# Pieces 0 to 3 of x loaded through ScalarE's DMA queue in a one-core decoder layer

## The chip, the cores and the metric

The kernel runs on 1 core of a Trainium2 chip. A core has a matrix engine (TensorE, PE in the profile), VectorE (DVE), ScalarE (ACT), GpSimd (POOL) and SyncE (SP), and DMA engines that all of them share. Each engine runs its own list of instructions in order, and the lists meet only through semaphores. A load is an instruction in the list of the engine that issues it; it finishes later, by itself, and raises a semaphore. The metric is the device time of one execution in microseconds, as the median of several runs.

## What is computed

One decoder layer over 256 tokens of width 2048, in float32. The start of it matters here: all of x is multiplied by the input weights, head by head.

```python
proj = jnp.einsum('bsd,dc->bsc', x, w_in[l]).astype(f32)       # x: (1, 256, 2048)
q_a, k_a, v_a, q_b, k_b, v_b = jnp.split(proj, splits, axis=-1)
q_a = apply_rope(q_a...); k_a = apply_rope(k_a...)
o_a = diff_attention(q_a, k_a, v_a, lam, subln_g[l], lambda_init)
...
o_b = dilated_attention(q_b, k_b, v_b)
attn_out = jnp.einsum('bsc,cd->bsd', mix, w_out[l])
x = layer_norm(DEEPNORM_ALPHA * x + attn_out, ln1_g[l], ln1_b[l])
hdn = jnp.square(jax.nn.relu(jnp.einsum('bsd,df->bsf', x, w_ff1[l])))
ff_out = jnp.einsum('bsf,fd->bsd', hdn, w_ff2[l])
x = layer_norm(DEEPNORM_ALPHA * x + ff_out, ln2_g[l], ln2_b[l])
```

## The kernel before

**Units.** The 2048 rows of a weight matrix are taken in 8 units of 256 rows (`KU` = 2 blocks of 128). For one head a unit is 256 x 384 numbers (q, k and v of the head), 384 KB, loaded by two instructions of 192 KB (L263). Units go round four buffers, `SLOTS` = 4, of `w_raw`. Unit k of head 0 is called unit k below; units 8 and up are the next head's.

**Three products for one.** To keep float32 precision each operand is split in a rounded part and a rest. ScalarE rounds `w_raw` to `w_hi` (L646), VectorE subtracts to get `w_lo` (L893), and TensorE adds three products, hi x hi, hi x lo, lo x hi (L366, L368, L370). A unit of a head takes 12 of them, for 2 blocks of rows and 2 tiles of tokens.

**x.** x comes in 8 pieces of 256 columns, 256 KB each (L277), into `y1`, which the profile calls `y`. TensorE transposes a piece by four instructions (`transpose_x`, L341) against the identity, itself a load of 64 KB at the very start (L1332). ScalarE rounds the transposed piece to `xT_hi` (L667) and VectorE makes `xT_lo` (L911). Unit k needs piece k.

**What sets the order.** The order is written out by hand. TensorE, in `head_slot`, first does 6 warm-up products on zeros (`WARM_UP`, L331), transposes piece 0, 2 warm-ups, piece 1, 2 warm-ups, then unit 0; then pieces 2 and 3, then unit 1; then one piece ahead of each of the next four units. ScalarE and VectorE take, in turn, piece k and unit k for the first four. A piece's bank of PSUM is used again four pieces later.

**SyncE's queue.** SP issues in turn: piece 0, unit 0, piece 1, unit 1 and so on to piece 7, unit 7. Units 0 to 3 wait for nothing. From unit 4 on, a unit's load waits for the semaphore `w_split`, raised when the unit four before it has been split (`load_head_unit`, L259). Whatever is behind it on SP waits too.

**GpSimd** starts its loads (`lam_in`, then `tables`, which the rope of L933 to L940 needs) once TensorE has finished unit 1. The first rope, its sum `qk` (L940) and the transposes of it on TensorE (L409) come in the second head's turn, after its unit 1.

**ScalarE's queue** issues no load at all in this version. Its first instruction loads the table of activation functions.

Of the kernel before, what the change touches and what calls it, by code (L numbers as in the profile page):

```python
# [20 lines left out]
P = 128  # L21
# [16 lines left out]
KU = 2  # L38
SLOTS = 4
# [65 lines left out]
def hybrid_layer(nc, x, w_in, lq1, lk1, lq2, lk2, subln_g, w_out, ln1_g, ln1_b, w_ff1, w_ff2,  # L105
# [5 lines left out]
    def at(name, shape, dtype, offset):  # L111
        return nc.alloc_sbuf_tensor_at(name, shape, dtype, offset=base + offset)
# [43 lines left out]
    y1 = at("y1", [P, TT, D_MODEL], F32, A0 + 24 * KB)  # L156
# [44 lines left out]
    def sem(name):  # L201
        sems[name] = nc.alloc_semaphore(name)
        return sems[name]
# [6 lines left out]
    x_loaded = [sem(f"x_loaded{k}") for k in range(UPH)]  # L210
# [27 lines left out]
    x_d = x.rearrange("b (t p) d -> p (b t) d", p=P)  # L238
# [16 lines left out]
    def load_head_unit(sp, kind, h, head, k, first_lap=False):  # L255

        slot = k % SLOTS
        if not first_lap:
            sp.wait_ge(w_split, UPH * h + k - (SLOTS - 1))  # L259
        dst = w_raw[:, slot, 0:KU * HC].rearrange("p (k s d) -> p k s d", k=KU, s=3)  # L260
        for kk in range(KU):
            src = w_in_d[:, k, kk, kind, :, one(head), :].rearrange("p s h d -> p s (h d)")
            sp.dma_start(dst[:, kk], src).then_inc(w_loaded[slot], 16)  # L263

    def load_chunk_unit(sp, w, u, row, chunk, slot, back=SLOTS):

        sp.wait_ge(w_split, u - (back - 1))
        dst = w_raw[:, slot, :].rearrange("p (k n) -> p k n", k=KU)
        src = w[:, row, :, chunk, :] if isinstance(chunk, int) else (
            w[:, row, :, one(chunk), :].rearrange("p k c n -> p k (c n)"))  # L270
        sp.dma_start(dst, src).then_inc(w_loaded[slot], 16)

    def sync_program(sp):

        for k in range(UPH):
            cols = slice(k * KU * P, (k + 1) * KU * P)
            sp.dma_start(y1[:, :, cols], x_d[:, :, cols]).then_inc(x_loaded[k], 16)  # L277
            load_head_unit(sp, 0, 0, 0, k, first_lap=k < SLOTS)
        for kind in range(2):
            first = 1 if kind == 0 else 0  # L280
            with sp.Fori(first, N_DIFF) as j:
                for k in range(UPH):
                    load_head_unit(sp, kind, j + N_DIFF * kind, j, k)
        with sp.Fori(0, CHUNKS - 1) as n:
            for k in range(UPH):
                load_chunk_unit(sp, w_out_d, UPH * n + (U_OUT + k), k, n, k % SLOTS)

        sp.wait_ge(w_used, U_OUT + UPH)
        for k in range(SLOTS):
            sp.dma_start(side_raw[:, k, :].rearrange("p (k n) -> p k n", k=KU),  # L290
                         w_ff1_d[:, k, :, 0, :]).then_inc(side_loaded[k], 16)
        for k in range(UPH):
            load_chunk_unit(sp, w_out_d, U_OUT + UPH * (CHUNKS - 1) + k, k, CHUNKS - 1, k % SLOTS)
        for k in range(SLOTS, UPH):
            load_chunk_unit(sp, w_ff1_d, U_FF1 + k, k, 0, k % SLOTS, back=2 * SLOTS)
        with sp.Fori(1, CHUNKS_FF) as n:
            for k in range(UPH):
                load_chunk_unit(sp, w_ff1_d, UPH * n + (U_FF1 + k), k, n, k % SLOTS)
        with sp.Fori(0, CHUNKS - 1) as n:
            with sp.Fori(0, UPF // SLOTS) as lap:  # L300
                for k in range(SLOTS):
                    load_ff2_unit(sp, UPF * n + SLOTS * lap + (U_FF2 + k), SLOTS * lap + k, n, k)
        for k in range(UPF):
            load_ff2_unit(sp, U_FF2 + UPF * (CHUNKS - 1) + k, k, CHUNKS - 1, k % SLOTS)
            if k == UPF * 3 // 4:

                sp.wait_ge(w_used, U_FF2 + UPF * (CHUNKS - 1) + UPF // 2)
                for n, v in enumerate((ln2_g, ln2_b)):
                    sp.dma_start(ln2_gb[:, n, :], v.partition_broadcast(P).rearrange(
                        "p l d -> p (l d)")).then_inc(gb2_loaded, 16)  # L310
        for i, (tt, cols) in enumerate(LAST_PIECES):
            sp.wait_ge(y2_ready, i + 1)
            sp.dma_start(out_d[:, tt, cols], y2[:, tt, cols]).then_inc(stored, 16)
        sp.wait_ge(stored, 16 * len(LAST_PIECES))

    def load_ff2_unit(sp, u, row, chunk, slot):
        sp.wait_ge(w_split, u - (SLOTS - 1))
        dst = w_raw[:, slot, :].rearrange("p (k n) -> p k n", k=KU)
        if isinstance(row, int):
            src = w_ff2_d[:, row, :, chunk, :]  # L320
        else:
            src = w_ff2_d[:, one(row), :, one(chunk), :].rearrange("p u k c n -> p (u k) (c n)")
        sp.dma_start(dst, src).then_inc(w_loaded[slot], 16)
# [310 lines left out]
    def scalar_program(act):  # L634
        def round_unit(u, slot, lap, cols, fresh=False, back=SLOTS, units=1):

            if cols == KU * HC:
                loads = KU * lap  # L640
            else:
                loads = lap + (KU - 1) * (U_OUT // SLOTS)
            act.wait_ge(w_loaded[slot], 16 * loads)
            if not fresh:
                act.wait_ge(w_used, u - (back - 1))
            act.activation(w_hi[:, slot, 0:cols], w_raw[:, slot, 0:cols], ACT.Copy).then_inc(  # L646
                w_rounded, units)
# [16 lines left out]
        def round_x(i):  # L664

            act.wait_ge(turned, i + 1)
            act.activation(xT_hi[:, i * KU:(i + 1) * KU, :].rearrange("p k t -> p (k t)"),  # L667
                           piece_ps[i % 4], ACT.Copy).then_inc(turn_rounded, 1)
# [34 lines left out]
        def scale_output(h):  # L703
            act.wait_ge(scale_ready, h + 1)
            for tt in range(TT):
                ins = act.activation(o_sb[:, tt, :], out_ps[:, 0, tt * P:(tt + 1) * P], ACT.Copy,
                                     scale=o_scale[:, tt:tt + 1])
            ins.then_inc(o_ready, 1)
# [12 lines left out]
        def slot(h, parity, att_maps, out_maps):  # L721
# [23 lines left out]
            if att_maps == 2:  # L745
                scale_output(h - 1)

        for k in range(SLOTS):
            round_x(k)
            round_unit(k, k, 1, KU * HC, fresh=True)  # L750
# [578 lines left out]
    with nc.Block() as block:  # L1329
        @block.sync  # L1330
        def _(sp):
            sp.dma_start(ident_t[:, :], table[:, 0:P]).then_inc(ident_loaded, 16)  # L1332
            sync_program(sp)

        @block.tensor
        def _(pe):
            tensor_program(pe)

        @block.scalar
        def _(act):  # L1340
            scalar_program(act)

        @block.vector
        def _(dve):
            vector_program(dve)

        @block.gpsimd
        def _(pool):
            gpsimd_program(pool)
# [19 lines left out]
```

## Time and profile before

| | us |
|---|---|
| median of 3 runs | 1130.5 |
| lowest and highest | 1129.39, 1130.81 |
| the profiled execution | 1129.92 |
| its span, first to last instruction | 1128.1 |
| TensorE busy with products | 1112.4 |
| VectorE busy | 654.3 |
| ScalarE busy | 506.2 |

Times in the profile count from the start of the span. A row of the view in order of time gives the start, the length, the engine, the line, what is written and read, and in brackets how long the engine had been idle and what ended it. `PEld` is TensorE's loading of the stationary operand, `SPq` SyncE issuing a load; the length of such a row is the issuing, not the transfer. Rows with x4 or x12 are merged from as many instructions. Matmuls are pipelined, so one row's length is more than its distance to the next.

### The profile page before, as it was taken

How to read it: one execution, taken by the hardware profiler on the slowest of the kernel's cores; microseconds unless marked ns; L12 is line 12 of the kernel's file. 1: busy time of each engine (PE TensorE's matmuls, PEld its weight loads, DVE VectorE, ACT ScalarE, POOL GpSimd, SP SyncE). 2: the span in 40 equal slices, each digit the busy share in tenths (PEclk: the TensorE clock that was granted, in tenths of full speed). 3: DMA queues.
4: the chain of work that ended last, by engine and by line, in shares of the span. 5: the costliest groups of instructions: out<-in, count | busy, mean ns of one | idle time of the engine just before them, and what ended most of it. 6: DMA issues, size and time to landing. Idle time of an engine off the chain costs nothing.

```text
span 1128.1 us, 16832 instructions
## 1 busy us (share of the span) xinstructions
PE 1112.4 (99%) x5884; PEld 981.6 (87%) x5884; DVE 654.3 (58%) x737; ACT 506.2 (45%) x676; POOL 25.6 (2%) x53
## 2 busy tenths in 40 slices
PE   9999999999999999999999999999999999999996
PEld 8999999999988878888888888888888888888885
DVE  5666666665655685566556555655445445445446
ACT  4555555444543434444445444444333343343341
POOL 1000000000000010000000000000000000000001
PEclk9999999999999999999999999999999999999998
DMA  9655557655565855666666666667666666656672
GB/s 264 187 154 165 166 167 229 180 162 175 164 201 170 282 173 163 188 188 187 199 187 186 187 190 191 182 195 263 198 194 191 197 190 193 197 190 194 193 264 93
DMA packets 185764, 215.42 MB, mean 191 GB/s; under 512 B 9281, under 2 KB 110017, under 8 KB 185089
## 3 DMA queue, kind: packets, MB, share of 16 engines
q1 hardware_dynamic: 184352, 207.72, 60.5%
q0 software_dynamic: 1376, 7.21, 1.9%
q8 instruction: 25, 0.41, 0.1%
q14 instruction: 11, 0.08, 0.0%
HBM read 210.70 MB, written 4.19 MB: 190 GB/s over the span
## 4 chain that ended last, share of the span: by engine, by line
PE 95%; DVE 2%; DMA 2%; issue 1%; SPq 0%; ACT 0%; POOL 0%; POOLq 0%; DVEq 0%
PE low_ps L574 11%; PE high_ps L370 10%; PE high_ps L368 10%; PE high_ps L366 10%; PE low_ps L366 10%; PE low_ps L370 10%; PE low_ps L368 10%; PE high_ps L574 9%; PE low_ps L579 5%; PE high_ps L579 5%; PE high_ps L419 1%; PE high_ps L442 1%; PE high_ps L409 1%; DMA w_raw<-in_w_in 1%; DMA y<-in_x 1%
## 5 line engine op out<-in xcount | busy, mean ns | idle before, releaser
L893 DVE TENSOR_TENSOR w_lo<-w_raw,w_hi 128x1024 fp32r<-128x1024 f32 (+1 forms) x408 | 462.5, 1140 | 373.0 <-ACT w_hi L646 372.5
L646 ACT ACTIVATE w_hi<-w_raw 128x1024 fp32r<-128x1024 f32 (+1 forms) x408 | 403.9, 992 | 495.9 <-PE high_ps L370 191.9
L366 PE MATMUL high_ps<-w_hi,hidT_hi 128*128 128x512 f32 x480 | 186.8, 389 | 0.0
L370 PE MATMUL high_ps<-w_hi,hidT_lo 128*128 128x512 f32 x480 | 186.8, 389 | 0.0
L368 PE MATMUL high_ps<-w_lo,hidT_hi 128*128 128x512 f32 x480 | 186.8, 389 | 0.0
L366 PE MATMUL low_ps<-w_hi,xT_hi 128*128 128x384 f32 x512 | 179.0, 350 | 0.0
L574 PE MATMUL low_ps<-x1T,w_hi 128*128 128x512 f32 x512 | 176.8, 394 | 0.7 <-ACT relu L830 0.7
L370 PE MATMUL low_ps<-w_hi,xT_lo 128*128 128x384 f32 x512 | 171.8, 336 | 0.0
L368 PE MATMUL low_ps<-w_lo,xT_hi 128*128 128x384 f32 x512 | 171.7, 335 | 0.0
L574 PE MATMUL high_ps<-x1T,w_hi 128*128 128x512 f32 x448 | 155.0, 394 | 0.0
L579 PE MATMUL low_ps<-x1T,w_lo 128*128 128x256 f32 x512 | 137.0, 278 | 0.0
L579 PE MATMUL high_ps<-x1T,w_lo 128*128 128x256 f32 x448 | 119.9, 278 | 0.0
L574 PEld LDWEIGHTS low_ps<-x1T,w_hi 128*128 128x128 f32 x512 | 94.4, 188 | 20.4 <-ACT relu L830 1.1
L368 PEld LDWEIGHTS high_ps<-w_lo,hidT_hi 128*128 128x128 f32 x480 | 90.1, 188 | 18.8
L366 PEld LDWEIGHTS high_ps<-w_hi,hidT_hi 128*128 128x128 f32 x480 | 90.1, 188 | 18.7
L370 PEld LDWEIGHTS high_ps<-w_hi,hidT_lo 128*128 128x128 f32 x480 | 90.1, 188 | 18.6
L366 PEld LDWEIGHTS low_ps<-w_hi,xT_hi 128*128 128x128 f32 x512 | 96.4, 188 | 3.1 <-issue 2.7
L579 PEld LDWEIGHTS low_ps<-x1T,w_lo 128*128 128x128 f32 x512 | 96.2, 188 | 2.8
L574 PEld LDWEIGHTS high_ps<-x1T,w_hi 128*128 128x128 f32 x448 | 82.6, 188 | 17.2
L368 PEld LDWEIGHTS low_ps<-w_lo,xT_hi 128*128 128x128 f32 x512 | 96.5, 188 | 0.2
L370 PEld LDWEIGHTS low_ps<-w_hi,xT_lo 128*128 128x128 f32 x512 | 96.1, 188 | 0.0
L579 PEld LDWEIGHTS high_ps<-x1T,w_lo 128*128 128x128 f32 x448 | 84.2, 188 | 2.5
(134 smaller groups left out, 810.0 us busy)
## 6 DMA issues: line engine op xcount, KB each, us to landing
w_raw<-in_w_ff SPq DMA_DIRECT2D x252, 512.0 KB, 3.7
w_raw<-in_w_in SPq DMA_DIRECT2D x256, 192.0 KB, 2.7
w_raw<-in_w_out SPq DMA_DIRECT2D x32, 512.0 KB, 4.8
y<-in_x SPq DMA_DIRECT2D x8, 256.0 KB, 5.5
side_raw<-in_w_ff SPq DMA_DIRECT2D x4, 512.0 KB, 6.9
ln_spill<-y POOLq DMA_DIRECT2D x8, 256.0 KB, 3.4
y<-ln_spill POOLq DMA_DIRECT2D x1, 2048.0 KB, 10.3
ln_gb<-in_ln_g POOLq DMA_DIRECT2D x1, 1024.0 KB, 6.1
```

The lines of the kernel that those rows point to most:

```text
L366: pe.matmul(acc[:, tt, 0:cols], hi[:, toks], right_hi[:, slot, w], start=(t == 0), stop=False)
L368: pe.matmul(acc[:, tt, 0:cols], hi[:, toks], right_lo[:, slot, w], start=False, stop=False)
L370: ins = pe.matmul(acc[:, tt, 0:cols], lo[:, toks], right_hi[:, slot, w], start=False, stop=(t == kts - 1))
L409: ins = pe.transpose(turn_ps[:, 0, s * SEQ + tt * P:s * SEQ + (tt + 1) * P], qk[:, tt, s * P:(s + 1) * P], ident_t[:, :])
L419: ins = pe.matmul(scores_ps[:, m, keys_of(tt)], qkT[rows, 0, tt * P:(tt + 1) * P], qkT[rows, 1, 0:(tt + 1) * P], start=True, stop=True)
L442: ins = pe.matmul(out_ps[:, 0, first:first + P], left, right, start=(key_tile == 0), stop=(key_tile == tt))
L574: return pe.matmul(banks[:, b, :], w_hi[:, slot, cols], x1T[:, t, :, :].rearrange("p h t -> p (h t)"), start=(t == 0), stop=(t == KT - 1))
L579: return pe.matmul(banks[:, b, 0:SEQ], w_lo[:, slot, cols], x1T[:, t, 0, :], start=False, stop=False)
L646: act.activation(w_hi[:, slot, 0:cols], w_raw[:, slot, 0:cols], ACT.Copy).then_inc(w_rounded, units)
L893: dve.tensor_tensor(w_lo[:, slot, 0:cols], w_raw[:, slot, 0:cols], w_hi[:, slot, 0:cols].bitcast(F32), ALU.subtract).then_inc(w_split, units)
```

## The change

The four loads of pieces 0 to 3 move from SyncE's list to the head of ScalarE's. SyncE issues units 0 to 3 one after the other and goes on with piece 4. All other instructions, waits and buffers stay; each piece still raises its own semaphore.

```diff
+    def load_x(queue, k):
+
+        cols = slice(k * KU * P, (k + 1) * KU * P)
+        queue.dma_start(y1[:, :, cols], x_d[:, :, cols]).then_inc(x_loaded[k], 16)
+
     def sync_program(sp):
 
         for k in range(UPH):
-            cols = slice(k * KU * P, (k + 1) * KU * P)
-            sp.dma_start(y1[:, :, cols], x_d[:, :, cols]).then_inc(x_loaded[k], 16)
+            if k >= SLOTS:
+                load_x(sp, k)
             load_head_unit(sp, 0, 0, 0, k, first_lap=k < SLOTS)
...
+        for k in range(SLOTS):
+            load_x(act, k)
         for k in range(SLOTS):
             round_x(k)
             round_unit(k, k, 1, KU * HC, fresh=True)
```

The start of SyncE's list, as a difference (- before, + after; `y_80` is the buffer of x, `x8` means eight such rows in a row; the lines of the changed kernel lie a few higher):

```order
-L1332 DMA ident_t<-in_table 128x128
-L277 DMA y_80<-in_x 128x2x256
+L1339 DMA ident_t<-in_table 128x128
+L263 DMA w_raw<-in_w_in 128x3x128 x8
+L276 DMA y_80<-in_x 128x2x256
 L263 DMA w_raw<-in_w_in 128x3x128 x2
-L277 DMA y_80<-in_x 128x2x256
+L276 DMA y_80<-in_x 128x2x256
```

The eight loads of units 0 to 3 now stand in one block behind the identity, and the first x on this list is piece 4.

The start of ScalarE's list before:

```order
L1339 UNCONDITIONAL_BRANCH
L667 ACT_TABLE_LOAD
L667 ACTIVATE xT_hi<-high_ps 128x512
L646 ACTIVATE w_hi<-w_raw 128x768
```

And after:

```order
L1346 UNCONDITIONAL_BRANCH
L276 DMA y_80<-in_x 128x2x256 x4
L672 ACT_TABLE_LOAD
L672 ACTIVATE xT_hi<-high_ps 128x512
L651 ACTIVATE w_hi<-w_raw 128x768
```

Four loads of x stand ahead of the table load; the rounding work behind it keeps its order. TensorE's, VectorE's and GpSimd's lists are the same.

## Rows read from the trace of the kernel before

**Rows 1.** The page: busy time of TensorE; shares of the last chain; the loads of x

```profile
PE 1112.4 (99%) x5884; PEld 981.6 (87%) x5884; DVE 654.3 (58%) x737; ACT 506.2 (45%) x676; POOL 25.6 (2%) x53
...
PE 95%; DVE 2%; DMA 2%; issue 1%; SPq 0%; ACT 0%; POOL 0%; POOLq 0%; DVEq 0%
...
y<-in_x SPq DMA_DIRECT2D x8, 256.0 KB, 5.5
```

**Rows 2.** The granted clock of the core over the whole span

```profile
core 0: 1128.1 us, clock 0.997
```

**Rows 3.** Waits of TensorE, whole program: us in total, times, longest

```profile
PE high_ps L341 <- DMA y<-in_x: 1.4, 2, 0.8
...
PE high_ps L409 <- DVE qk L940: 0.9, 1, 0.9
```

**Rows 4.** In order of time, 0 to 20 us: TensorE, ScalarE, VectorE

```profile
1.06 2.93 PE L331 MATMUL low_ps<-zeros 128*128 128x128 f32 x12 [1.06 <-DVE zeros L1019]
...
4.82 1.09 PE L341 MATMUL high_ps<-ident_t,y 128*128 128x128 f32 x4 [0.83 <-DMA y<-in_x]
...
6.43 0.83 ACT L646 ACTIVATE w_hi<-w_raw 128x768 fp32r<-128x768 f32 x1
...
6.86 1.12 PE L341 MATMUL high_ps<-ident_t,y 128*128 128x128 f32 x4
7.30 0.96 DVE L893 TENSOR_TENSOR w_lo<-w_raw,w_hi 128x768 fp32r<-128x768 f32 x1
...
8.48 0.55 PE L366 MATMUL low_ps<-w_hi,xT_hi 128*128 128x384 f32 x1
...
9.02 0.85 ACT L646 ACTIVATE w_hi<-w_raw 128x768 fp32r<-128x768 f32 x1 [0.41 <-DMA w_raw<-in_w_in]
...
10.78 0.60 PE L341 MATMUL high_ps<-ident_t,y 128*128 128x128 f32 x4
...
11.90 0.66 PE L341 MATMUL high_ps<-ident_t,y 128*128 128x128 f32 x4 [0.53 <-DMA y<-in_x]
...
12.32 0.42 PE L366 MATMUL low_ps<-w_hi,xT_hi 128*128 128x384 f32 x1
...
19.54 0.60 PE L341 MATMUL high_ps<-ident_t,y 128*128 128x128 f32 x4
```

**Rows 5.** In order of time: ScalarE's first instruction and SyncE's issues

```profile
0.74 1.28 ACT L667 ACT_TABLE_LOAD   x1 [0.74 <-PEq L1360]
...
1.18 0.42 SPq L277 DMA_DIRECT2D y<-in_x  x1
1.65 0.99 SPq L263 DMA_DIRECT2D w_raw<-in_w_in  x2
...
12.54 0.90 SPq L277 DMA_DIRECT2D y<-in_x  x1
```

**Rows 6.** The last chain, 0 to 45 us: start, length, what

```profile
5.84 6.02 DMA y<-in_x
...
20.67 0.84 ACT w_hi L646
...
23.22 7.09 DMA w_raw<-in_w_in
...
34.22 0.66 PE high_ps L409 x4
```

**Rows 7.** Piece 0 alone (issued 1.18): time from issue to landing

```profile
DMA to landing us min/median/max: 3.5/3.5/3.5
```

**Rows 8.** Unit 0's two loads (issued 1.65 and 2.16): the second landed last

```profile
DMA to landing us min/median/max: 3.2/3.4/3.6
```

**Rows 9.** Unit 1's second load alone, issued 3.73

```profile
DMA to landing us min/median/max: 5.3/5.3/5.3
```

**Rows 10.** Queues, 22.5 to 25.5 us: packets, MB, share; q0 is GpSimd's, q1 SyncE's

```profile
q0 software_dynamic: 157, 0.66, 57.5%
q1 hardware_dynamic: 760, 0.37, 43.0%
```

## The prediction

> **What bounds the kernel now.** I read the page first: TensorE has work in 99% of the span and makes 95% of the chain that ended last, while transfers make 2% [rows 1]. A change to loads can therefore only act where TensorE waits for one. The waits of TensorE come next: for pieces of x there are two in the whole program, 1.4 us together, the longer one 0.8; later there is one of 0.9 us for `qk`, the result of the first rope [rows 3]. Then the start in order of time [rows 4], where the reader should see two meeting paths. One is x: its piece 0 is transposed at 4.82, piece 1 at 6.86, then warm-up products, and the first product of unit 0 comes at 8.48. The other is the weights: unit 0 is rounded by ScalarE at 6.43 and split by VectorE from 7.30 to 8.26. They arrive within 0.2 us of each other, so either one alone can delay unit 0. Unit 0 then runs until 10.78. Piece 2 is transposed at once, piece 3 only at 11.90, since it landed at 11.86 [rows 6], and unit 1 starts at 12.32. From there each unit follows the last without a wait (such transposes come at 19.54, for piece 6). So what can be won before unit 1 is the wait for piece 3; the earlier wait, 0.8 us before 4.82, lies ahead of a path that has to be kept short on both sides.
>
> **The clock at the start.** The granted clock reads 0.997 over the span [rows 2]. The lengths are plainer: four transposes take 1.09 and 1.12 us at 4.82 and 6.86, and 0.60 at 10.78 [rows 4]. TensorE is at the lower of its two levels (1.2 GHz) until about 8.4 and at 2.4 GHz after it, having been busy most of the time since 1.06.
>
> **What the change takes away.** SP no longer issues pieces 0 to 3, four instructions of 0.42 us (piece 0's) to 0.5 (half of the 0.99 for two weight loads), 1.7 to 2.0 us in all [rows 5]. Nothing computes on SP, and its issuing runs ahead of the landing: piece 3 is issued at 5.84 and lands 6.02 us later [rows 6], piece 0 lands 3.5 us after its issue [rows 7]. The saved issue time is thus worth only the start. Unit 0's two loads, issued from 1.65, can start at about 1.2; piece 0, issued at 1.18, can start at 0.74, where ScalarE's first instruction stands [rows 5]. That is a lead of 0.44 us.
>
> **What it adds.** ScalarE issues four loads ahead of its table load. At SP's own 0.5 us each that is 2.0 us; the table load of 1.28 us then ends at 4.0 instead of 2.0 [rows 5]. ScalarE's first work, rounding piece 0, comes after the transposes, about 5.9, so 1.9 us of cover remain. It is gone if one issue takes over 0.98 us. A gain is excluded, since no later work starts sooner by it. I count 0.
>
> **What it moves: whose bytes come first.** The same bytes are loaded. Units carry 384 KB, pieces of x 256 KB, the identity 64. From the landings before: 704 KB (identity, piece 0, unit 0) at 2.16 + 3.6 = 5.8 [rows 8]; 1344 KB (with piece 1 and unit 1) at 3.73 + 5.3 = 9.0 [rows 9]; 2240 KB (with piece 2, unit 2, piece 3) at 11.86. Between these I interpolate, 196 and 317 KB per us. Now two queues are full at once and share the DMA engines. How they share is not in the start of this trace. The nearest rows are those where GpSimd's queue and SP's are both full, 22.5 to 25.5: 157 packets with 0.66 MB against 760 packets with 0.37 MB, 57.5% against 43.0% of the engines' time [rows 10]. The number of packets is far from equal, the time is nearly so. I take equal bytes for x (packets of 1 KB) and weights (512 B), with the 0.44 us of lead:
> - Unit 0 ends its queue's first 448 KB, so 896 KB in all: 6.74 - 0.44 = 6.3. ScalarE rounds it at 6.43 as before: no delay.
> - Piece 1 ends 512 KB of x, 1024 KB in all: 7.4 - 0.44 = 7.0 against 6.86. Unit 0's first product moves by 0.1 to 8.6, its end to 10.9.
> - Piece 3 ends x, by then 832 to 1024 KB of weights may be in too: at most 1856 to 2048 KB, 10.2 to 10.8 instead of 11.86. It no longer makes TensorE wait. The two sets of transposes, 0.35 and 0.42 us (10.78 and 11.90 show such sets; 11.90 to 12.32 is one), follow unit 0: unit 1 can start at 11.7.
> - Unit 1 is through with 1664 to 1856 KB: 9.6 to 10.2 against 9.0, later. Rounding 0.85 and splitting 0.96 [rows 4] with 0.1 between put its split at 11.5 to 12.1. This is what is late next, in place of piece 3.
> So unit 1 starts at 11.7 to 12.1 instead of 12.32: **0.2 to 0.6 us earlier; I take 0.5**, near the equal shares.
>
> **The queue behind the waits.** Pieces 4 to 7 stay on SP, each in front of a unit that waits for an earlier split. Unit 5 waits for unit 1's split, which moves from 10.9 to about 11.5 or 12, and piece 6 is queued behind it. Piece 6 was issued at 12.54 [rows 5], pieces take a median 5.5 us to land [rows 1], and its transposes came at 19.54 [rows 4]: 1.5 us of slack, of which the later issue takes 0.6 to 1.2 and the earlier TensorE 0.5. I count 0, up to +0.3. Piece 4 is issued earlier than before, behind the same bytes: 0.
>
> **What becomes of it.** The next stretch in which TensorE waits is at 34.22, 0.9 us for the rope [rows 3], whose chain runs through a weight load of 7.09 us [rows 6]. If that chain doesn't come forward, TensorE waits longer there and the gain is gone: between 0 and -0.5. The chain begins with the rounding at 20.67 [rows 6], which follows the transposes of a piece of x, and GpSimd's loads start at the end of unit 1, so both move with TensorE; I keep -0.5. Of a delay the same wait could swallow up to 0.9. After that no load is waited for by TensorE [rows 3], so the shift goes to the end.
>
> **Sum.** The profiled execution took 1129.92 us (span 1128.1). 1129.92 - 0.5 = 1129.4. That execution lies 0.6 below the median of the three runs, so the median should be 1130.0.
>
> The Trainium skill speaks against the change: DMA: Bandwidth & Descriptors, section Rules for kernel authors, says that spreading loads over the issuing engines doesn't raise bandwidth and saves issue time alone. Where issue time isn't waited for, that gives no change, 1130.5; the trace agrees that it isn't waited for, but the order of the bytes is another matter, and on that my half microsecond rests.
>
> **Rivals.**
> *A, the loads still come in order of issue.* Then the change hardly does what it says: unit 0's second load stands behind two or three pieces, 960 to 1216 KB, 6.6 to 7.9. From rounding to first product it took 8.48 - 6.43 = 2.05, so unit 0 starts at 8.7 to 9.9, ends 2.3 later, and after 0.8 of transposes unit 1 starts at 11.8 to 13.0; with unit 1 landed at 10.2 not before 12.1. That is -0.2 to +0.7: 1130.3 to 1131.2. For it: every row of the start shows that order on one queue. Against it: rows 10.
> *B, slower: x crowds out unit 0.* If the queues take turns by packets of equal number, x gets two bytes for each byte of weights. Unit 0 lands behind 448 KB and 896 KB of x: 9.0 - 0.44 = 8.6. It starts at 10.65 (+2.2), unit 1 at 13.8 (+1.5). From about 8.4 to 10.65 TensorE then has nothing to do, directly at the point where its clock rises. With the clock up this is +0.6 (0.9 swallowed) to +1.5: 1131.1 to 1132.0. If it is down for unit 0, the twelve products that take 2.3 us (8.48 to 10.78) take twice that, +2.3: +2.9 to +3.8, or 1133.4 to 1134.3. The mechanism begins once unit 0 lands after 6.4, and costs over 0.2% when it also takes the clock. For it: the wait for both paths leaves no slack. Against it: the counts of rows 10, one to five.
> The skill's same page, section Queues, rings and completion order, has each DMA engine take turns between queues packet by packet; read as equal counts of descriptors that is B's time, while rows 10 show the counts unequal.
> *C, faster:* two queues fill the engines sooner. Without the waits of 0.8 and 0.5 us, and with the lead, at best -1.3: 1129.2. No step here reaches -2.3.
>
> **How the numbers follow.** This kernel can be told from no change at about 0.2%, 2.3 us. Chances: forecast 0.45; A 0.25; B with the clock up 0.13; B with it down 0.12; C 0.02, and 0.03 for something in the start that I don't see. Same takes the forecast, A, C and B with the clock up, 0.85, less 0.03 for a larger gain than I see: 0.82. Slower is B with the clock down and two thirds of the unseen, 0.14. Faster is that 0.03 and the last third, 0.04. The likeliest gives 1130.0, its own bounds (0 to -0.6, medians of three runs differing by some 0.7) 1129.2 to 1131.2. The range leaves out the lower clock: 1128.8 to 1132.4.
>
> **What would show it.** Right: pieces 0 to 3 on ScalarE from 0.74; no wait for x before the transposes of piece 3; unit 0's first product at 8.4 to 8.7; unit 1's at 11.7 to 12.1, held by VectorE's split; the wait for the rope still 0.8 to 1.0. Wrong: ScalarE rounding unit 0 after 7 us because of a transfer (A or B), first products of 0.35 us spacing instead of 0.17 (the clock), or the rope's wait taking up the shift.

## The result

| | before | changed |
|---|---|---|
| median of 15 runs each, us | 1130.5 | 1132.11 |
| lowest and highest | 1129.1, 1131.65 | 1130.87, 1134.44 |
| ratio, 95% interval | | 1.0019 (1.0012 to 1.0026) |
| profiled execution, its span | 1129.92, 1128.1 | 1133.35, 1131.6 |

The changed kernel is 1.6 us slower; a gain of 0.5 was predicted. It was measured twice more, later: 1.0003 (0.9993 to 1.0012, which holds no change) and 1.0015 (1.0005 to 1.0024). So the loss lies between 0.6 and 1.6 us by the medians and between 0.3 and 2.1 by the ratios, and a difference that small needs many runs. In two of the three measurements its executions also spread more than those of before.

The start of the changed kernel in order of time, to be laid beside [rows 4] and [rows 5] (start, length, engine, line, operation, what ended the idle time; `ACTq` is ScalarE issuing):

```profile
0.73 2.04 ACTq L276 DMA_DIRECT2D y<-in_x  x4
...
1.18 6.80 SPq L263 DMA_DIRECT2D w_raw<-in_w_in  x8
2.81 1.28 ACT L672 ACT_TABLE_LOAD   x1 [2.81 <-issue]
...
4.39 1.09 PE L346 MATMUL high_ps<-ident_t,y 128*128 128x128 f32 x4 [0.41 <-DMA y<-in_x]
...
6.63 0.66 PE L346 MATMUL high_ps<-ident_t,y 128*128 128x128 f32 x4 [0.42 <-DMA y<-in_x]
...
7.12 0.61 PE L336 MATMUL low_ps<-zeros 128*128 128x128 f32 x4
...
8.50 0.84 ACT L651 ACTIVATE w_hi<-w_raw 128x768 fp32r<-128x768 f32 x1 [2.38 <-DMA w_raw<-in_w_in]
...
9.38 0.96 DVE L900 TENSOR_TENSOR w_lo<-w_raw,w_hi 128x768 fp32r<-128x768 f32 x1 [2.54 <-ACT w_hi L651]
...
10.48 0.66 PE L371 MATMUL low_ps<-w_hi,xT_hi 128*128 128x384 f32 x1 [2.75 <-DVE w_lo L900]
...
11.26 0.52 PE L375 MATMUL low_ps<-w_hi,xT_lo 128*128 128x384 f32 x1
...
11.58 0.52 PE L371 MATMUL low_ps<-w_hi,xT_hi 128*128 128x384 f32 x1
...
14.46 1.89 PE L346 MATMUL high_ps<-ident_t,y 128*128 128x128 f32 x8
...
16.02 0.50 PE L371 MATMUL low_ps<-w_hi,xT_hi 128*128 128x384 f32 x1
```

Three things differ from [rows 4]. First, ScalarE waits 2.38 us for unit 0 and rounds it at 8.50 instead of 6.43. Second, TensorE therefore stands idle for 2.75 us until 10.48 (before: 8.48, no wait). Third, the products of unit 0 come 0.32 us apart (11.26 to 11.58), not 0.17, so the unit takes until 14.46: 4.0 us instead of 2.3. The two sets of transposes behind it wait for nothing, as intended, but at the slow rate they take 1.56 us. Unit 1 begins at 16.02 instead of 12.32, **3.7 us later**.

TensorE's clock by stretch (the column after the five engines is the granted clock, 1.00 being 2.4 GHz; then the share of the DMA engines and GB/s):

```profile
5.00:10.00 5.00, 2.32 (x15) 1.94 (x13) 1.31 (x2) 1.93 (x3) 0.00 (x0) 0.94 1.07 307
10.00:15.00 5.00, 4.52 (x15) 4.45 (x16) 1.89 (x3) 0.84 (x1) 0.00 (x0) 0.50 1.10 302
15.00:20.00 5.00, 5.00 (x31) 4.97 (x30) 3.59 (x5) 3.65 (x6) 0.93 (x2) 0.88 0.46 137
```

Here the column shows it: 0.50, the lower level, from 10 to 15 us. The transposes of piece 1 at 6.63 took 0.66 us, so the clock had already been up, and it fell while TensorE was idle: 0.94 over 5 to 10 us is 0.6 us at the lower level, which puts the fall near 9.4, some 1.7 us after the last product on zeros. The column must be read with care. It reads 1.00 from 0 to 5 us too, where four transposes took 1.09 us, and in e9 from 10 to 15 us, where products are 0.32 us apart: the trace has no record of the clock before its first change, which in e9 is the rise at 13.6 us. The spacing of the products is the surer sign.

The waits of TensorE, against [rows 3]: us in total, times, longest.

```profile
PE low_ps L371 <- DVE w_lo L900: 3.1, 2, 2.7
...
PE high_ps L346 <- DMA y<-in_x: 0.8, 2, 0.4
...
PE high_ps L414 <- DVE qk L947: 0.3, 1, 0.3
```

The wait for x shrank from 1.4 to 0.8, the new wait for unit 0's split is 2.7, and the rope's wait gave back 0.6 (0.9 to 0.3), half of which a new 0.3 us wait for a split shortly before it (at 33.09) took again. The profiled execution grew by 3.4 us. So nearly the whole shift of unit 1 reached the end.

### The profile page after: what moved, and what is told of

Same layout as the page of the kernel before. It is cut to its first block, busy times and chain, and to the rows that moved or that the text cites. A ratio compares the mean times of both kernels' runs of the same rounds, so it can differ in the third digit from the quotient of the medians.

```text
span 1131.6 us, 16832 instructions
## 1 busy us (share of the span) xinstructions
PE 1114.2 (98%) x5884; PEld 983.3 (87%) x5884; DVE 654.1 (58%) x737; ACT 506.4 (45%) x676; POOL 25.6 (2%) x53
## 4 chain that ended last, share of the span: by engine, by line
PE 95%; DVE 2%; DMA 2%; issue 1%; ACT 0%; POOL 0%; SPq 0%; POOLq 0%; DVEq 0%
PE low_ps L579 10%; PE low_ps L371 10%; PE high_ps L373 10%; PE high_ps L371 10%; PE high_ps L375 10%; PE low_ps L375 10%; PE low_ps L373 10%; PE high_ps L579 9%; PE low_ps L584 5%; PE high_ps L584 5%; DMA w_raw<-in_w_in 1%; PE high_ps L424 1%; PE high_ps L447 1%; PE high_ps L414 1%; DMA w_raw<-in_w_out 0%
```

## The experiments

All kernels ran beside the kernel before on the same chip. In the table, "rounded" is when ScalarE starts on unit 0, "first" TensorE's first product of unit 0, "spacing" the distance of its products, "unit 1" the first product of unit 1, all from the profile of one execution; the ratio is of many runs (7 to 15 of each version).

| kernel | rounded | first | spacing | unit 1 | span | ratio (95%) |
|---|---|---|---|---|---|---|
| before | 6.43 | 8.48 | 0.17 | 12.32 | 1128.1 | 1 |
| changed | 8.50 | 10.48 | 0.32 | 16.02 | 1131.6 | 1.0019 (1.0012, 1.0026) |
| changed again, e9 | 8.65 | 10.64 | 0.32, late 0.17 | 14.95 | 1131.4 | 1.0003 (0.9993, 1.0012) |
| changed, e12 | 8.09 | 10.07 | 0.32, late 0.17 | 14.56 | 1129.7 | 1.0015 (1.0005, 1.0024) |
| x first, one queue, e1 | 9.82 | 11.80 | 0.32 | 16.32 | 1131.6 | 1.0032 (1.0020, 1.0043) |
| changed, more warm-up, e2 | 7.66 | 9.64 | 0.18 | 12.62 | 1128.3 | 0.9999 (0.9990, 1.0009) |
| the same, e13 | 7.72 | 9.70 | 0.17 | 12.65 | 1128.2 | 0.9997 (0.9988, 1.0006) |
| changed, no warm-up, e14 | 7.25 | 9.23 | 0.32 | 14.12 | 1128.8 | 1.0021 (1.0011, 1.0031) |
| x in 512 B rows, e3 | 7.29 | 9.38 | 0.32 | 14.26 | 1132.3 | 1.0018 (1.0009, 1.0028) |
| x in 8 loads, 1 KB rows, e4 | 7.39 | 9.37 | 0.18 | 13.31 | 1129.1 | 1.0001 (0.9991, 1.0010) |
| weights on ScalarE, e6 | 8.89 | 10.87 | 0.32 | 16.41 | 1132.5 | 1.0023 (1.0013, 1.0032) |
| x3 before unit 2, e7 | 5.92 | 7.89 | 0.17 | 11.46 | 1127.4 | 0.9999 (0.9990, 1.0009) |
| before, no warm-up, e8 | 5.74 | 8.68 | 0.32 | 13.58 | 1129.4 | 0.9997 (0.9988, 1.0007) |
| two pieces, e5 | 6.79 | 8.77 | 0.18 | 11.74 | 1127.2 | 0.9993 (0.9984, 1.0003) |
| two pieces again, e10 | 6.75 | 8.73 | 0.17 | 11.70 | 1127.7 | 1.0000 (0.9991, 1.0009) |
| two pieces, 4 warm-ups, e11 | 6.83 | 8.81 | 0.17 | 11.76 | 1126.4 | 0.9994 (0.9985, 1.0003) |
| the same, e15 | 6.98 | 8.97 | 0.17 | 11.92 | 1128.1 | 0.9991 (0.9982, 1.0000) |

### The changed kernel once more

> The changed kernel once more, on the same chip and in the same rounds as the two below. Theory (late unit 0 plus, in part of the executions, the lower clock): unit 0 lands at 7.6 to 8.6, behind three pieces of x; median 1131.5 to 1132.5, spread over 3 us, as before. Rival (the first measurement was a matter of the chip): median within 0.5 us of the kernel before.

Unit 0 landed at 8.63, at the edge of what was expected, but the median of 11 runs, 1131.1, was only 0.6 above the kernel before in those rounds, and the interval holds no change. Both the theory's range and the rival's were missed by a little. The executions lay from 1129.8 to 1133.2, those of before from 1128.9 to 1132.4, so no single profile stands for the median.

### Order or queue: x first on one queue

```diff
+        for k in range(SLOTS):
+            load_x(k)
         for k in range(UPH):
-            cols = slice(k * KU * P, (k + 1) * KU * P)
-            sp.dma_start(y1[:, :, cols], x_d[:, :, cols]).then_inc(x_loaded[k], 16)
+            if k >= SLOTS:
+                load_x(k)
             load_head_unit(sp, 0, 0, 0, k, first_lap=k < SLOTS)
```

> The kernel before, still with SyncE's queue alone, but with pieces 0 to 3 of x issued ahead of units 0 to 3. It puts the order of the bytes apart from the second queue. Theory (unit 0 is late because bytes of x come ahead of it): unit 0 stands behind 64 + 1024 KB, 1472 KB with itself, lands near 9.4 us, and its first product comes near 11.5; TensorE is idle for over 3 us before it, its clock is at the lower level for unit 0, and the time is 1133 to 1135. Rival (it is the second queue that costs, by contention or by ScalarE's issuing): unit 0 lands by 7 us or the time stays within 0.5 us of 1130.5.

The theory held. Without any second queue, unit 0 landed at 9.80 and the time was 0.32% above the kernel before, the worst of all.

```profile
9.82 0.84 ACT L652 ACTIVATE w_hi<-w_raw 128x768 fp32r<-128x768 f32 x1 [4.09 <-DMA w_raw<-in_w_in]
...
11.80 0.66 PE L372 MATMUL low_ps<-w_hi,xT_hi 128*128 128x384 f32 x1 [4.75 <-DVE w_lo L899]
```

It is thus enough that bytes of x come ahead of unit 0.

### How the two queues share: size of packets or size of loads

```diff
+        if k < SLOTS:
+            for c in range(KU):
+                half = slice((k * KU + c) * P, (k * KU + c + 1) * P)
+                queue.dma_start(y1[:, :, half], x_d[:, :, half]).then_inc(x_loaded[k], 16)
```

(the wait becomes 32 for these pieces; the control splits by `tt` instead: `y1[:, tt, cols]`, rows of 1 KB)

> The changed kernel, with each of pieces 0 to 3 loaded by two instructions of 128 columns, so that x comes in packets of 512 B as the weights do. Theory (the two queues take turns by something close to packets, and x wins by its larger ones): x and weights get equal bytes while both queues are full, unit 0 lands near 6.5 to 7.2 instead of 8.5, time 1130.0 to 1131. Rival (turns by instruction or by bytes): packet size changes nothing, unit 0 lands near 8.5 as in the changed kernel. The table load on ScalarE ends near 6.1 instead of 4.1, which may hold the rounding of piece 0 by 0.6 us.

> Control of the run with 512 B packets: each of pieces 0 to 3 is loaded by two instructions as well, one for each tile of tokens, with packets of 1 KB as in the changed kernel. Theory (packets): x gets more bytes than the weights, unit 0 lands at 8.0 to 8.6 and the time is as the changed kernel's, near 1132. Rival (the number of instructions or ScalarE's slower issue decides): unit 0 lands as early as in the run with 512 B packets.

The theory of packets fell. Queue lines for 3 to 6 us (packets, MB, share of the DMA engines; q10 is ScalarE's queue with x, q1 SyncE's with the weights), first of the changed kernel:

```profile
q10 hardware_dynamic: 533, 0.52, 53.9%
q1 hardware_dynamic: 747, 0.37, 45.3%
```

With x in loads of 128 KB and packets of 512 B:

```profile
q1 hardware_dynamic: 908, 0.45, 52.2%
q10 hardware_dynamic: 619, 0.30, 37.6%
```

With x in loads of 128 KB and packets of 1 KB:

```profile
q1 hardware_dynamic: 1017, 0.50, 57.8%
q10 hardware_dynamic: 405, 0.37, 39.6%
```

The bytes of x to those of the weights are 1.4, 0.67 and 0.74 to 1. The sizes of one load of each are 256 to 192 (1.33), 128 to 192 (0.67) and 128 to 192. The size of a packet, doubled between the last two, moved little. The shares follow the size of a load, as if the queues took turns load by load. With the queues exchanged (e6, below) they still do over the same 3 us: x, now on q1, has loads of 256 KB and 1.6 times the bytes.

```profile
q1 hardware_dynamic: 521, 0.50, 56.9%
q10 hardware_dynamic: 646, 0.32, 36.3%
```

Both engines issue a load in 0.49 us, one after the other, so turns by load can't be told here from plain order of issue.

Shares alone don't give the landing. A load raises its semaphore sixteen times, and the trace holds the time of each. Of the 32 signals of unit 0's two loads, the 24th came at 5.16 us in the kernel before and at 6.2 to 6.4 in the six profiles with the changed kernel's loads. The last one, which is the landing, came at 5.80 before and at 7.2 to 8.6 in those six. In the changed kernel's own profile 31 of the 32 had come by 6.79 and the last at 8.48, after piece 2 (7.68). With two pieces on ScalarE's queue (e5) the 24th came at 5.95 and the last at 6.76. So about 1.1 us of the late landing is in the bulk of the bytes, and the rest, 0.2 to 1.7 us, differs from execution to execution and lies in the last few signals. What delays those is not shown.

Both expectations missed in part. With 512 B rows unit 0 landed at 7.19, as its theory said, but the median was 1132.87 instead of 1130 to 1131. In the control it landed at 6.42 instead of 8.0 to 8.6, so its rival held; ScalarE rounded it only at 7.39, since it had issued eight loads and its table load ended at 6.9.

The medians are a different matter: with 512 B rows the time was no better than the changed kernel's, although unit 0 was rounded at 7.29. Piece 1 landed at 7.7 there and was transposed at 7.75, the table load ended late (6.8), and unit 0 ran at the lower clock. A version can cure one delay and meet another.

### The queues exchanged

```diff
+        for k in range(SLOTS):
+            load_head_unit(act, 0, 0, 0, k, first_lap=True)
         for k in range(SLOTS):
             round_x(k)
```

> The queues exchanged: units 0 to 3 (8 loads of 192 KB) on ScalarE's queue, all pieces of x on SyncE's. Theory (turns by whole load, whichever engine issues): order of landing as in the changed kernel, unit 0 near 7.7 to 8.5. ScalarE now issues 8 loads, over 4 us, so its table load ends after 6 us and the rounding of piece 0 begins near 6.5: time 1131 to 1134. Rival (SyncE's queue is served last, ScalarE's first): unit 0 lands by 6 us.

Right in the time, wrong in the landing. Unit 0's halves were now the first and third load to be issued and landed by 6.4; no engine's queue is served last. What held unit 0 in this profile was ScalarE itself, which issued for 6.34 us before it could load its table:

```profile
0.73 6.34 ACTq L263 DMA_DIRECT2D w_raw<-in_w_in  x8
7.11 1.28 ACT L668 ACT_TABLE_LOAD   x1 [7.11 <-issue]
8.40 0.60 ACT L668 ACTIVATE xT_hi<-high_ps 128x512 fp32r<-128x512 f32 x1
8.89 0.84 ACT L647 ACTIVATE w_hi<-w_raw 128x768 fp32r<-128x768 f32 x1
```

The last three of these loads took 0.8 to 1.6 us to issue instead of 0.5: the cover that the prediction counted for ScalarE's issues does run out, with eight loads.

### The clock: work for TensorE in the wait

```diff
-WARM_UP = (6, 2, 2)
+WARM_UP = (6, 2, 9)
```

> The changed kernel with 9 warm-up products on zeros ahead of unit 0 instead of 2, so that TensorE has work until about 9.5 us. Theory (part of the loss is TensorE's clock, which falls during the wait for unit 0): unit 0's products stand 0.17 us apart instead of 0.32, its first product stays near 10.5, and the median is 1131.0 to 1131.5, with no run over 1133. Rival (the loss is the late landing alone, the clock only goes with it): spacing or median unchanged within 0.3 us of 1132.1, or worse by the products added.

> The changed kernel, beside the next two. Theory (landing alone costs 0.3 to 0.8 us at the end, the clock up to 2 more in part of the executions): median 0.5 to 1.6 us above the kernel before. Rival (landing alone): all executions 0.3 to 0.8 us above it.

> The changed kernel with 9 instead of 2 warm-up products ahead of unit 0. Theory (clock): median at least 0.5 us below the changed kernel's in the same rounds, and the slowest executions, over 1132.5, gone. Rival (no clock): as the changed kernel, or slower.

> The changed kernel with no warm-up products at all, so that TensorE does nothing but two sets of transposes until unit 0 at about 10.5 us. Theory (clock): all of unit 0 and often part of unit 1 at the lower level in every execution, median 1132.5 to 1134, 1 us or more above the changed kernel. Rival: no different from the changed kernel, as the kernel before showed no difference without its warm-up.

The first run showed the loss gone, but in another session than the changed kernel's. e12, e13 and e14 ran side by side. Medians: 1131.51, 1129.95 and 1132.31, beside 1130.2 for the kernel before. The slowest executions were 1135.8, 1130.6 and 1134.5. Seven useless products more make the changed kernel 1.6 us faster. Without any, e14 was only 0.8 us above e12, less than the 1 us and more that was expected. With the seven, of e13:

```profile
6.11 0.66 PE L346 MATMUL high_ps<-ident_t,y 128*128 128x128 f32 x4 [0.25 <-DMA y<-in_x]
...
6.60 2.17 PE L336 MATMUL low_ps<-zeros 128*128 128x128 f32 x18
...
7.72 0.84 ACT L651 ACTIVATE w_hi<-w_raw 128x768 fp32r<-128x768 f32 x1 [1.67 <-DMA w_raw<-in_w_in]
...
9.70 0.41 PE L371 MATMUL low_ps<-w_hi,xT_hi 128*128 128x384 f32 x1 [0.93 <-DVE w_lo L900]
10.12 0.34 PE L375 MATMUL low_ps<-w_hi,xT_lo 128*128 128x384 f32 x1
10.30 0.33 PE L371 MATMUL low_ps<-w_hi,xT_hi 128*128 128x384 f32 x1
...
12.65 0.42 PE L371 MATMUL low_ps<-w_hi,xT_hi 128*128 128x384 f32 x1
```

Unit 0 is still 1.2 us late (9.70), its products are 0.17 us apart, and unit 1 is only 0.3 late, since it no longer waits for piece 3. That is the price of the order of bytes alone, and by the ratio of 0.9997 it can't be told from nothing. The rest of the loss goes with the clock, whether it falls in the wait or hasn't risen by then: in e9 and e12 the transposes of piece 1, at 6.7 and 6.8, still took 1.12 us. e12, the same loads without the added products, has unit 1 at 14.56, 1.9 later:

```profile
6.79 1.12 PE L346 MATMUL high_ps<-ident_t,y 128*128 128x128 f32 x4 [0.63 <-DMA y<-in_x]
```

But the two profiles differ before the added products begin. The kernels are the same up to there, and yet in e13 (and e2) the clock was already up at 6.11, in e12 not at 6.79. So the pair shows what the two states of the clock are worth, 1.9 us at unit 1. That the products keep it up is shown by the medians and the slowest executions, and once more by e10 and e11 below (two and four products, medians 1130.1 and 1129.4), not by these profiles. The profiled execution of e14 was its fastest run (1130.54), which is why its span looks better than its ratio.

The Trainium skill (TensorE: Matmul & The Clock Gate, section What's actually happening) has the array throttled by default, at half its clock, until activity releases it. The trace agrees in the two levels: spacings of 0.32 and 0.17 us.

> The kernel before, all loads as they were, without any of the warm-up products on zeros. It puts the price of TensorE's clock apart from the landings. Theory (of the changed kernel's loss some 2 us are the clock): unit 0 lands as before, its products stand 0.32 us apart, unit 0 takes 4.0 us instead of 2.3 and perhaps part of unit 1 too, time 1131.5 to 1133. Rival (the clock costs little, since the wait for piece 3 and the rope's wait take it up): within 0.5 us of 1130.0.

The kernel before without its warm-up products (`WARM_UP = (0, 0, 0)`): in the profile unit 0 ran at the lower clock and unit 1 began 1.3 us late, the wait for piece 3 having swallowed the rest. The profiled execution took 1131.27, but the median was that of the kernel before (1130.3 to 1130.2): the rival held, not the theory of 1131.5 to 1133.

```profile
7.92 1.12 PE L341 MATMUL high_ps<-ident_t,y 128*128 128x128 f32 x4 [2.70 <-DMA y<-in_x]
8.68 0.67 PE L366 MATMUL low_ps<-w_hi,xT_hi 128*128 128x384 f32 x1
...
13.58 0.42 PE L366 MATMUL low_ps<-w_hi,xT_hi 128*128 128x384 f32 x1
```

Why the median doesn't show the 1.3 us stays open: one profile doesn't say how often the clock is down, in either kernel. It is the one run that speaks against a price of the clock.

### Is the gain to be had without the loss?

> The kernel before with SyncE's queue alone and one exchange: piece 3 of x is issued ahead of unit 2 instead of behind it. It asks whether the gain that the change was predicted to make (no wait for piece 3 after unit 0) is to be had without touching unit 0. Theory (landing in order of issue): unit 0 as before, first product near 8.5; piece 3 lands behind 1856 KB, near 10.7, so its transposes follow piece 2's at once and unit 1 starts near 11.7 instead of 12.32, time 0.3 to 0.6 us below the kernel before. Rival: unit 2, now later, or the rope's wait at 34 us takes it up and the time is unchanged.

On one queue, with piece 3 issued ahead of unit 2:

```profile
11.46 0.42 PE L372 MATMUL low_ps<-w_hi,xT_hi 128*128 128x384 f32 x1
...
14.45 0.66 PE L347 MATMUL high_ps<-ident_t,y 128*128 128x128 f32 x4 [0.66 <-DMA y<-in_x]
14.86 0.42 PE L372 MATMUL low_ps<-w_hi,xT_hi 128*128 128x384 f32 x1
```

Unit 1 began at 11.46, 0.9 earlier. Of this 0.6 is not the exchange: unit 0 had begun at 7.89 instead of 8.48, with the clock already up for piece 0 (its transposes took 0.63 us). Then TensorE waited for piece 4, and unit 2 began at 14.86 (kernel before: 14.84). The gain was turned into the next wait, and the median didn't move. The rival was right.

> The changed kernel with only pieces 0 and 1 on ScalarE's queue; pieces 2 and 3 go back to SyncE, ahead of units 2 and 3. The runs so far show landings in turns of whole loads, one from each queue: piece 0, first half of unit 0, piece 1, (piece 2,) second half of unit 0. Theory (turns by whole load): with no piece 2 on that queue, unit 0 is whole behind 64 + 512 + 384 = 960 KB and lands near 6.6 to 7.1 instead of 7.7 to 8.5; first product near 9.0, clock up in most executions, median 1129.8 to 1130.8. Rival (any second queue delays unit 0 as much): landing near 8, median near 1132.

> Pieces 0 and 1 on ScalarE's queue, 2 and 3 on SyncE's, for an interval that can tell 0.8 us. Theory: unit 1 begins at 11.7 instead of 12.3 and the shift goes to the end, 0.5 to 0.9 us below the kernel before. Rival: the first 0.8 us was noise or is taken up by the rope's wait, and the difference is under 0.3 us.

> The same with 4 instead of 2 warm-up products before unit 0, in the 1.1 us in which TensorE waits for unit 0's split. Theory (the clock still falls there in some executions): fewer slow executions, median 0.2 to 0.5 us lower than with two. Rival: with landing near 6.8 the clock holds anyway, and four products at the lower clock take 2.1 us and delay unit 0 by 0.3 us: same or up to 0.3 us more.

> Pieces 0 and 1 on ScalarE, 4 warm-up products ahead of unit 0, once more. Theory: 0.5 to 1.0 us below the kernel before. Rival: within 0.3 us of it.

```diff
-            if k >= SLOTS:
+            if k >= 2:
                 load_x(sp, k)
...
-        for k in range(SLOTS):
+        for k in range(2):
             load_x(act, k)
```

With pieces 0 and 1 alone on ScalarE's queue (e5):

```profile
6.79 0.84 ACT L651 ACTIVATE w_hi<-w_raw 128x768 fp32r<-128x768 f32 x1 [0.48 <-DMA w_raw<-in_w_in]
...
8.77 0.41 PE L371 MATMUL low_ps<-w_hi,xT_hi 128*128 128x384 f32 x1 [1.15 <-DVE w_lo L900]
...
11.74 0.42 PE L371 MATMUL low_ps<-w_hi,xT_hi 128*128 128x384 f32 x1
...
14.29 0.42 PE L371 MATMUL low_ps<-w_hi,xT_hi 128*128 128x384 f32 x1
```

This is the timing that the prediction gave the full change: unit 1 at 11.7, and unit 2 at 14.3, 0.55 ahead of the kernel before, so in this profile the gain outlasts the next unit. In the time it isn't shown: two measurements gave 0.9993 and 1.0000, both intervals hold no change, and the second is what its rival said. With two more warm-up products (e11, e15) it was 0.9994 and 0.9991 (0.9982 to 1.0000). By the ratios that last version is 0.7 to 1.0 us faster than the kernel before (medians 1129.4 and 1129.2 against 1130.5 and 1130.2), at the edge of what can be told.

## Why the prediction was right or wrong

1130.0 was predicted and 1132.11 measured: inside the range of 1128.8 to 1132.4, but in the other direction. That it lies inside is owed to the rivals that the range took in, since the forecast's own mechanism allowed no loss, and in part to luck: the lower clock, which the profiles show, was left out of it.

- **What bounds the kernel, and where a load can act:** right. Nearly all of the difference was made before unit 1. That nothing of slack lay between unit 0's landing and its first product was right too, and proved to be the decisive row.
- **ScalarE's cover for four issues:** right. They took 2.04 us together and the table load ended at 4.1; with eight loads (e6) the cover was gone.
- **How two full queues share the DMA engines:** this is the step that failed. From [rows 10] equal bytes for both queues were taken, which gave unit 0's landing as 6.3 and no delay. It landed at 7.2 to 8.6 in six profiles with these loads. The rows don't even say so: their time is nearly equal, 57.5% to 43.0%, but their bytes are 0.66 to 0.37, 1.8 to 1. They were also of another pair of queues, with packets and loads of other sizes. In the changed kernel the time was nearly equal too (53.9% to 45.3%) and the bytes 1.4 to 1 for x. Put into the prediction's own interpolation, 448 KB of weights and 627 KB of x give 7.2; what comes on top, up to 1.4 us, goes with the late last signals, for which the prediction had no term. The runs put rival A's order in its place: one load of x, then one of the weights, by turns or by order of issue.
- **TensorE's clock:** the forecast kept it up, by way of a unit 0 that isn't late, and gave it to rival B alone. In the profile 2.0 us of the shift at unit 1 come from the later start and 1.7 from unit 0 at the lower level, and the two sets of transposes at that level used up what the wait for piece 3 would have given back (1.56 us against 1.54 with the wait).
- **Piece 3 no longer waited for:** right in all profiles of the changed kernel, and its worth was sized right with the clock up: in e13, 1.2 us late at unit 0 becomes 0.3 at unit 1.
- **Rival A** gave unit 1 at 11.8 to 13.0 and 1130.3 to 1131.2. With the clock held up it was 12.6. Its landing, 6.6 to 7.9, was 0.6 to 0.7 too early at the ends. It kept the lead of 0.44 us, which the landings show for piece 0 (4.26 against 4.68) and hardly for piece 1 (6.58 against 6.81); the rest isn't explained.
- **Rival B** had the wrong mechanism, packets taking equal turns, and the right consequence. Its first product at 10.65 and its +2.9 to +3.8 with the clock down stand against 10.48 and +3.4 (1133.35 less 1129.92); that they agree so well is luck, with the mechanism wrong. A late landing of any cause opens the wait in which the clock falls or doesn't rise. The chance of 0.12 for the lower clock was tied to the packets, and so probably too low. In the profiles of the changed kernel's start with its own warm-up, three of three had unit 0 wholly or mostly at the lower level; how often an execution has, no run counts.
- **What becomes of a shift:** the 0.9 us wait of the rope was to swallow part of a delay. It shrank by 0.6, and a new wait in front of it took 0.3, so 3.4 of 3.7 us arrived. Even in e7 a gain was lost at the very next wait and not there.

## What to carry to other kernels

Moving loads to a second queue doesn't only save issue time. It decides anew whose bytes come first, and a load for which two engines stand ready can be pushed back by loads that nobody waits for yet. Move only as many as are wanted before it: here four pieces cost up to 1.6 us and two cost nothing. Where TensorE must wait near its start, ask what its clock does there. Here the late bytes alone cost nothing in the median once seven useless products filled the wait (1129.95 against 1130.2), and 1.3 us without them (1131.51).

## What the runs showed of the hardware

- Two queues, ScalarE's and SyncE's, shared the DMA engines roughly in proportion to the size of their loads: 1.4, 0.67 and 0.74 to 1 for 256, 128 and 128 KB against 192 KB, and 1.6 to 1 for 256 KB with the queues exchanged. Halving the packet from 1 KB to 512 B changed little. Turns by load and plain order of issue weren't told apart.
- A load has landed with the last of its sixteen signals, and that one can come late. Of the 32 of unit 0's two loads, 31 had come by 6.79 us and the last at 8.48 in the changed kernel; in e14 it was 7.15 and 7.23.
- Together they moved no more than one queue does: 307 and 302 GB/s in the changed kernel's second and third 5 us, against 304 and 311 before. The Trainium skill (DMA: Bandwidth & Descriptors, Rules for kernel authors) says so of all issuing engines; here the trace agrees.
- Issuing a load of x or the weights took 0.42 to 0.49 us on either engine at first. Later it took up to 1.6 us on ScalarE (e6) and 2.6 on SyncE (e14).
- TensorE's clock, already up at 6.63 us (four transposes in 0.66 us), was down again at 10.48 after 2.75 us of idleness, and it stayed down through 5.5 us of dense work, to 16.02. With 1.15 us of idleness (e5) it stayed up.
- The same start of a kernel can find the clock in either state: at piece 1's transposes it was up in e2 and e13 (0.66 us for four) and in the changed kernel's first profile, and down in e9 and e12 (1.12 us).
